# Rotary angles and the rotary key of the last block computed through PSUM banks

## The reference, cut to what matters

```python
h = h + 0.5 * swiglu(rms_norm(h, g[2]), ffn_w_in[1, 1], ffn_w_out[1, 1])   # f3_in, f3_dn
...
proj = einsum(rms_norm_2(h, norm_mix_g), w_in)
qa, ka, va, c_q, c_kv, k_rope = split(proj)
kv = rms_norm_2(c_kv, ckv_norm_g) @ w_ukv                                   # b_ukv
kb = rms_norm_2(concatenate([k_nope, k_rope], -1), knorm_b_g)
kb = concatenate([kb[..., :64], apply_rope(kb[..., 64:], positions)], -1)

def apply_rope(x, positions):
    ang = positions[..., None] * inv_freq          # cos(ang), sin(ang)
    return concatenate([x1 * cos - x2 * sin, x2 * cos + x1 * sin], -1)
```

## Time and profile before

| | |
|---|---|
| median of 3 runs | 1642.77 us (1642.22 to 1649.35) |
| the profiled execution | 1645.47 us |
| its span in the trace | 1643.7 us |
| mean granted TensorE clock | 0.982 of full speed |
| TensorE (PE) busy | 1573.4 us, 96% of the span |
| VectorE (DVE) busy | 672.0 us, 41% |
| ScalarE (ACT) busy | 775.1 us, 47% |
| GpSimd (POOL) busy | 1132.3 us, 69% |

### The profile page before, as it was taken

One profiled execution on the slowest core, in us unless ns is written; L12 is line 12 of the kernel. 1 busy time (PEld: TensorE's weight loads), 2 busy tenths in 40 slices (PEclk: granted clock), 3 DMA queues, 4 the chain that ended last, 5 costly groups with the idle time before them and its releaser, 6 DMA issues.

```text
span 1643.7 us, 40794 instructions
## 1 busy us (share of the span) xinstructions
PE 1573.4 (96%) x16206; PEld 1498.6 (91%) x16206; DVE 672.0 (41%) x1533; ACT 775.1 (47%) x1271; POOL 1132.3 (69%) x835
## 2 busy tenths in 40 slices
PE   6999989899989999999999999999989999999998
PEld 6999989688878999999999997699989978699998
DVE  4332068664546433223332257643351455433200
ACT  5444446842324544445444443664445534555532
POOL 6777858683506777778777784088868964468885
PEclk9999999898899999999999999999999999999999
DMA  6544523310012544465444541065535533235541
GB/s 255 174 177 138 179 106 132 129 66 3 2 54 100 182 168 152 155 205 189 172 144 165 188 164 44 2 241 197 179 124 190 194 110 105 98 108 192 189 181 77
DMA packets 37910, 231.34 MB, mean 141 GB/s; under 512 B 4527, under 2 KB 6680, under 8 KB 16552
## 3 DMA queue, kind: packets, MB, share of 16 engines
q1 hardware_dynamic: 36552, 228.57, 39.5%
q10 hardware_dynamic: 1248, 1.24, 0.2%
HBM read 228.67 MB, written 2.63 MB: 141 GB/s over the span
## 4 chain that ended last, share of the span: by engine, by line
PE 87%; DVE 5%; POOL 3%; issue 2%; ACT 1%; DMA 0%; SPq 0%; DVEq 0%; POOLq 0%; ACTq 0%
PE PS L770 72%; POOL wlo L724 3%; PE PS L769 1%; PE PS L1001 1%; PE PS L1008 1%; PE PS L1016 1%; PE PS L1378 1%; DVE krot L2354 1%; PE PS L1166 1%; PE PS L1157 1%; PE PS L785 0%; PE PS L1040 0%; PE PS L1046 0%; DMA raw<-w_f_in_in 0%; PE PS L991 0%
## 5 line engine op out<-in xcount | busy, mean ns | idle before, releaser
L724 POOL TENSOR_TENSOR wlo<-raw,whi 128x256 fp32r<-128x256 f32 (+2 forms) x759 | 1085.5, 1459 | 452.9 <-ACT whi L2521 425.5
L770 PE MATMUL PS<-xh,whi 128*128 128x272 f32 (+1 forms) x2336 | 676.1, 289 | 22.4 <-POOL wlo L724 16.9
L770 PE MATMUL PS<-xl,whi 128*128 128x272 f32 (+1 forms) x2336 | 668.0, 286 | 0.0
L770 PE MATMUL PS<-xh,wlo 128*128 128x272 f32 (+1 forms) x2336 | 667.5, 286 | 0.0
L2521 ACT ACTIVATE whi<-raw 128x1024 fp32r<-128x1024 f32 x472 | 459.2, 981 | 386.7 <-PE PS L770 362.6
L770 PEld LDWEIGHTS PS<-xh,whi 128*128 128x128 f32 x2336 | 440.1, 188 | 31.6 <-issue 22.6
L770 PEld LDWEIGHTS PS<-xl,whi 128*128 128x128 f32 x2336 | 441.3, 189 | 0.6
L770 PEld LDWEIGHTS PS<-xh,wlo 128*128 128x128 f32 x2336 | 441.7, 189 | 0.0
L770 PE MATMUL PS<-hid_h,whi 128*128 128x272 f32 (+1 forms) x960 | 274.6, 286 | 5.4 <-POOL wlo L724 5.4
L770 PE MATMUL PS<-hid_h,wlo 128*128 128x272 f32 (+1 forms) x960 | 274.6, 286 | 0.0
L770 PE MATMUL PS<-hid_l,whi 128*128 128x272 f32 (+1 forms) x960 | 273.7, 285 | 0.0
(11 more groups left out here) (388 smaller groups left out, 1594.4 us busy)
## 6 DMA issues: line engine op xcount, KB each, us to landing
raw<-w_f_in_in SPq DMA_DIRECT2D x88, 1024.0 KB, 4.8
raw<-w_f_dn_in SPq DMA_DIRECT2D x64, 704.0 KB, 4.0
raw<-w_b_ff_in SPq DMA_DIRECT2D x32, 1024.0 KB, 4.8
raw<-w_rk_k_in SPq DMA_DIRECT2D x4, 1024.0 KB, 4.8
raw<-w_rk_r_in SPq DMA_DIRECT2D x4, 1024.0 KB, 4.8
raw<-w_rk_v_in SPq DMA_DIRECT2D x4, 1024.0 KB, 4.9
raw<-w_rk_o_in SPq DMA_DIRECT2D x4, 1024.0 KB, 4.8
raw<-w_at_q_in SPq DMA_DIRECT2D x4, 1024.0 KB, 5.1
```

Source lines behind the costliest of these rows:

```text
L724: last = nc.gpsimd.tensor_tensor(wlo[U % SPL][:, piece], raw[U % RAW][:, piece], whi[U % SPL][:, piece].bitcast(F32), ALU.subtract)
L770: mm(out, a, b, start=start and n == 0, stop=stop and n == 2, **kw)
```

## The change

The three intermediate arrays of the angles go to PSUM banks 4, 5 and 6 in place of SBUF (`ang`, `turns_ps`, `red`); only the rounded number of turns is still written to SBUF (`posf`). The first of these instructions waits for VectorE's own last low part of `f3`, since banks 4 to 7 held the gates. For the key, a copy of the gained key is written to the upper half of bank 3, by one instruction more than before and behind one more wait (for the latent's last low part, which read bank 3), and the cosine product reads that copy. Two SBUF arrays go away, and what lies behind them in SBUF moves down by 2 KB.

```diff
-        ang = tb("ang", [128, SEQ])
-        red = tb("red", [128, SEQ])
...
+            ang, turns_ps, red = PS[:, 4, 0:SEQ], PS[:, 5, 0:SEQ], PS[:, 6, 0:SEQ]
+
             def angle_begin():
                 dve.wait_ge(s_bc, 80)
-                step(v.tensor_copy(posf[:, :], posi[:, :]))
-                step(v.tensor_scalar(ang[:, :], posf[:, :], freq[:, 0:1], None, ALU.mult))
+                dve.wait_ge(s_hlo, HB["f3"] + FC)
+                step(v.tensor_copy(turns_ps, posi[:, :]))
+                step(v.tensor_scalar(ang, turns_ps, freq[:, 0:1], None, ALU.mult))
 
             def angle_turns(n):
-                step(v.tensor_scalar(posf[:, :], ang[:, :], 1 / (2 * math.pi), (0.25, 0.0)[n], ALU.mult, ALU.add))
-                step(v.tensor_scalar(posf[:, :], posf[:, :], MAGIC, None, ALU.add))
-                step(v.tensor_scalar(posf[:, :], posf[:, :], MAGIC, None, ALU.subtract))
+                step(v.tensor_scalar(turns_ps, ang, 1 / (2 * math.pi), (0.25, 0.0)[n], ALU.mult, ALU.add))
+                step(v.tensor_scalar(turns_ps, turns_ps, MAGIC, None, ALU.add))
+                step(v.tensor_scalar(posf[:, :], turns_ps, MAGIC, None, ALU.subtract))
 
             def angle_reduced(n):
-                step(v.scalar_tensor_tensor(red[:, :], posf[:, :], -C1, ang[:, :], ALU.mult, ALU.add))
+                step(v.scalar_tensor_tensor(red, posf[:, :], -C1, ang, ALU.mult, ALU.add))
                 for part in (C2, C3):
-                    step(v.scalar_tensor_tensor(red[:, :], posf[:, :], -part, red[:, :], ALU.mult, ALU.add))
+                    step(v.scalar_tensor_tensor(red, posf[:, :], -part, red, ALU.mult, ALU.add))
 
             def angle_end(n):
-                step(v.tensor_scalar(red[:, :], red[:, :], (math.pi / 2, 0.0)[n], PI, ALU.add, ALU.min))
-                v.tensor_scalar(cs_b[:, n, :], red[:, :], -PI, None, ALU.max).then_inc(s_ang, 1)
+                step(v.tensor_scalar(red, red, (math.pi / 2, 0.0)[n], PI, ALU.add, ALU.min))
+                v.tensor_scalar(cs_b[:, n, :], red, -PI, None, ALU.max).then_inc(s_ang, 1)
...
             step.do(v.tensor_tensor(kr[:, :], PS[:, G % 2, 0:SEQ], rstd[:, 0:SEQ], ALU.mult))
+            dve.wait_ge(s_x, X0["ckv"] + 1)
+            step.do(v.scalar_tensor_tensor(PS[:, 3, SEQ:2 * SEQ], PS[:, G % 2, 0:SEQ], col(VEC["kb_r"]), rstd[:, 0:SEQ], ALU.mult,
+                                           ALU.mult))
             v.scalar_tensor_tensor(kg[:, :], PS[:, G % 2, 0:SEQ], col(VEC["kb_r"]), rstd[:, 0:SEQ], ALU.mult,
                                    ALU.mult).then_inc(s_free, 1)
...
-            step(v.tensor_tensor(krot[:, :], kg[:, :], cs_b[:, 0, :], ALU.mult))
+            step(v.tensor_tensor(krot[:, :], PS[:, 3, SEQ:2 * SEQ], cs_b[:, 0, :], ALU.mult))
```

## The result

The changed kernel takes 1634.56 us in the median of 7 runs (1629.98 to 1638.21), the kernel before 1643.89 (1642.22 to 1649.88, 7 runs). The ratio is 0.9935, 95% interval 0.9917 to 0.9954: 0.65% faster, 10.7 us with an interval of 7.6 to 13.6. Forecast were 1631.0 and 11.8 us less. A second timing on another occasion gave 0.9941 (0.9920 to 0.9961). The profiled execution of the changed kernel has the longest time of the seven, 1638.21 us, with a span of 1636.4.

What follows compares the result with a forecast made beforehand. The kernel was taken as bound by TensorE's matmuls (72% of the span). Gains of 6.1 us (angles) and 5.7 (key), 11.8 together, took the profiled 1645.47 to 1633.7; run medians lie 2.7 lower, so 1631.0, range 1627 to 1637.5.

Steps and rivals of the forecast that it cites:

- No wait for POOL with PSUM on one side: Angle steps and line 2354: VectorE instructions with PSUM operands never wait for POOL; lines 1773 and 2321 peak at 450 and 490 ns.
- The chain of 18: VectorE's angle instructions in PSUM: 8.35 us in place of 12.3, bounds 7.6 to 9.5.
- the rule of the Trainium skill: At the angles: PSUM source costs 120 fixed cycles against 58, f32 loses the doubled rate; saving 1.15 us smaller.
- The pause and the clock: TensorE before unit 4: pause 1.7 us instead of 5.5, saving 3.8; full clock adds 2.3; 6.1 in all.
- Rival 1: At the angles: the clock falls although the pause is short; gain 9.5 us, time 1633.3; chance 0.20.
- The key: Line 2354 takes 0.42 us, the added copy costs nothing, TensorE's wait for `b_ka`'s drain goes; gain 5.7 us, bounds 4.0 to 5.8.
- Given back: Later stages: their clock pattern can add or take about 2 us, allowed for in the range.
- the distance from `b_keys(1)` to the end grows: Behind the key: a sign that the forecast is wrong; no size given.
- Rival 4: Last block: a new phase makes a VectorE instruction wait or lowers the clock; half the gain, 1637; chance 0.10.
- The sum: Whole kernel: 6.1 us at the angles plus 5.7 at the key, 11.8 us less; bounds 6.7 to 12.7.

Runs made afterwards that it cites:

- the longer chain: Changed kernel with seven more PSUM steps behind the angles, results unused; stretch at the angles 91.75 us against the changed kernel's 85.80.
- the gap: Kernel before, with POOL waiting for the rotated key ahead of its split of `b_va`; ratio 0.9973 to the kernel before.
- the run with long pieces: Kernel before, POOL splitting `b_ka`, `b_ukv`, `b_va` in pieces of 1024 columns instead of 256; one timed execution 1633.96 us beside 1640.03 before.

## Why the prediction was right, point by point

**No wait for POOL with PSUM on one side.** Right. It rested on the maxima of lines 1773 and 2321; in the changed profile no angle step exceeds 0.49 us and `krot` takes 0.42. The instructions that took the waits before are the same ones that lost them.

**The chain of 18.** Forecast 8.35 us from the step of 0.46 in the earlier trace rows, measured 8.37. The estimate by the rule of the Trainium skill that I set against it ("VectorE: DVE Perf Modes", the TRN2 errata) gave 1.15 us less gain; one-input steps went from 0.29 to 0.43, a gap of 0.14 and not 0.20, and the measurement decides for the rows.

**The pause and the clock.** Forecast a pause of 1.7 us at the full clock, measured 1.64 at 1.00. TensorE restarts 18.68 us after the first cut point before and 14.96 after, 3.7 earlier (forecast 3.8). The rest of the stretch's 5.73 is 2.0 for the clock, which I had put at 2.3: from the first to the 43rd matmul behind the pause the kernel before took 7.11 us and the changed one 5.08, where I had set 7.27 against 5.0. That the clock would stay up behind so short a pause was assumed, not worked out. It held in all five profiles with a pause of 1.64 or none, and the longer chain, with a long pause again, has the clock at 0.50 again. Rival 1 had no case in any profile of the changed kernel.

**The key.** Forecast 5.7, measured 5.52, the same to 0.01 us in all eight profiles with the product short or let in early. The added copy costs nothing, as the idle time behind it shows. The section of the Trainium skill ("SBUF — State Buffer", on who interferes with whom) names two kinds of instruction, those with two SBUF inputs and those in a two-port mode. Here instructions with two SBUF inputs and SBUF-to-SBUF ones with a single input were both blocked; no run shows in which mode the latter ran. That the loser waits for the other's one instruction fits the waits at the angles, but not the one at the key: there the instruction waited through the whole train of pieces and got in at the gap.

**Given back.** The term that I left at zero in the sum, with 2 us in the range, measured 1.28 up to the first score in the first pair: a stretch at the lower clock fell on other matmuls. It is not a constant price. The two columns behind the key sum to 301.2 and 304.0 in the profiles of before, to 302.4 and 303.8 in those of the changed kernel. One of my signs of being wrong, that the distance from `b_keys(1)` to the end grows, thus appeared in the first pair (1.2 us) and not in the second (0.2 less). Rival 4 happened in a small way at most, by the clock and not by a new wait, and cannot be told from what the kernel does by itself.

**The sum.** 11.8 forecast, 10.05 and 10.8 in the two pairs of traces, 10.7 and 9.7 by the two timings. The parts add up in the traces. In the timings they give 2.5 or 4.6 for the angles and 4.4 for the key, 7 to 9 together, against 9.7 to 10.7 for both at once; the intervals, 2.5 to 3.5 us each way, allow them to add up, and at the same granted clock they do. What stays open is a smaller thing: the angles alone timed at 2.4 and 3.6 there, where their shorter pause is 3.7, and of the clock's 2.0 only 1.0 and 1.3 show in their mean clock (0.9819 both times, against 0.9811 and 0.9808 before). There was luck in the forecast's closeness: the executions of one kernel spread over 8 to 15 us, and the forecast median, 1631.0, was worked out from a 3-run median that came out 1.1 us higher with 7 runs; the measured one is 3.6 us above it.

**Ahead of the angles.** The first 1208.6 to 1217.9 us differ by up to 9 us among fourteen profiles whose instructions there are the same. That is more than either edit is worth alone. In the first pair it is 2.75 us against the change, so that with the rest the profiled spans differ by 7.3 us only.

## What to carry to other kernels

Where GpSimd works in back-to-back pieces, look in VectorE's rows for one instruction that lasts many times its siblings. Give it a PSUM operand, or leave a gap in the train. Cutting GpSimd's work into short pieces can do the opposite of what it seems to: four pieces of 256 columns take 2.78 us where one of 1024 takes 2.40, and the pauses vanish. An SBUF-to-SBUF scalar operation with one input waited as well (1.80, 0.99 and 1.05 us in place of 0.29), so count both ends and not only the inputs. Price such a wait by what TensorE stands for behind it, and add the matmuls that run at the lower clock once the pause gets long: a pause of 1.6 us cost none, those of 4.0 to 5.4 cost 1.5 to 2.7 us more. Before a difference of a few us between two executions is explained, compare their granted clocks.

## What the runs showed of the hardware that I had not expected

A VectorE instruction with two SBUF inputs waited 9.5 us through fourteen POOL instructions of 0.70 us each, although a new one started every 0.70; with a gap it had ended 0.3 us after the last piece. At the angles the instructions of 1 to 2.5 us ended 0.15 to 0.3 us after the piece in hand, of 1024 or 384 columns, two of them when the next piece had already started. Why pieces of 256 columns shut VectorE out for a whole train stays open: the run with long pieces had pauses and didn't test it.

Splitting a weight unit earlier lengthened VectorE's chain by 2.75 us, because POOL then worked where it had been idle. An engine that is let go sooner can cost another one its quiet time.
